# A two-stack transformer kernel on one core: the second stack's attention goes from single heads in loops to pairs of heads, unrolled

## The reference

```python
def mla_attend(q_nope, q_rope, k_nope, k_rope, v):
    s = jnp.einsum('bqhd,bkhd->bhqk', q_nope, k_nope) + jnp.einsum('bqhr,bkr->bhqk', q_rope, k_rope)
    p = jax.nn.softmax(s.astype(jnp.float32) * SOFTMAX_SCALE, axis=-1).astype(v.dtype)
    return jnp.einsum('bhqk,bkhd->bqhd', p, v)
# q: rms_norm(c_q) @ w_q_b   (384 -> 12 heads x 96, of which 32 get a rotary turn)
# k, v: rms_norm(c_kv) @ w_kv_b   (128 -> 12 heads x (64 + 64)), the 32 rotary rows of k are shared
mix_l = jnp.concatenate([four_l, att_l], axis=-1) @ w_out[l]   # four_l: 2-D DFT of 256 channels
```

## Time and profile before

| | us |
|---|---|
| median of three runs | 3974.38 (3973.16 to 3976.8) |
| profiled execution, its own time | 3969.17 |
| its span | 3967.4 |
| TensorE busy | 3636.3 (92%) |
| VectorE busy | 2221.1 (56%) |
| ScalarE busy | 1364.0 (34%) |
| GpSimd busy | 190.7 (5%) |
| mean granted TensorE clock | 0.956 |

### The profile page before, as it was taken

One profiled execution on the slowest core, in us unless ns is written; L12 is line 12 of the kernel. 1 busy time (PEld: TensorE's weight loads), 2 busy tenths in 40 slices (PEclk: granted clock), 3 DMA queues, 4 the chain that ended last, 5 costly groups with the idle time before them and its releaser, 6 DMA issues.

```text
span 3967.4 us, 53234 instructions
## 1 busy us (share of the span) xinstructions
PE 3636.3 (92%) x19180; PEld 2914.2 (73%) x19180; DVE 2221.1 (56%) x3260; ACT 1364.0 (34%) x2104; POOL 190.7 (5%) x157
## 2 busy tenths in 40 slices
PE   8988999999998899999967998899999879879997
PEld 6755787888786578788846775688888657657876
DVE  7864456445686544744566553563535665545445
ACT  5544433222445443322212334142323233324322
POOL 2300000000230000000000000000000000000000
PEclk9988999999998999999978998999999989989998
DMA  3233332222223323222211001111111110112221
GB/s 131 85 139 120 115 113 100 96 95 95 85 86 139 139 100 113 98 95 98 94 58 53 22 21 49 43 53 64 64 64 64 54 64 22 49 64 85 93 87 74
DMA packets 44792, 325.32 MB, mean 82 GB/s; under 512 B 5088, under 2 KB 5344, under 8 KB 6112
## 3 DMA queue, kind: packets, MB, share of 16 engines
q1 hardware_dynamic: 43920, 315.88, 21.9%
q10 hardware_dynamic: 720, 7.40, 0.5%
HBM read 321.16 MB, written 2.10 MB: 81 GB/s over the span
## 4 chain that ended last, share of the span: by engine, by line
PE 76%; DVE 12%; ACT 5%; issue 3%; DVEq 3%; DMA 1%; ACTq 0%; SPq 0%
PE psum L663 10%; PE psum L665 10%; PE psum L664 10%; PE psum L1000 10%; PE psum L1002 10%; PE psum L1001 10%; PE psum L1113 3%; PE psum L1088 3%; ACT whi L1223 2%; PE psum L1099 2%; DVE wlo L1616 2%; DVE MA L1743 2%; PE psum L704 2%; PE psum L767 1%; PE psum L719 1%
## 5 line engine op out<-in xcount | busy, mean ns | idle before, releaser
L1223 ACT ACTIVATE whi<-wst 128x2048 fp32r<-128x2048 f32 x248 | 473.7, 1910 | 787.2 <-PE psum L1002 384.2
L1616 DVE TENSOR_TENSOR wlo<-wst,whi 128x2048 fp32r<-128x2048 f32 x216 | 495.0, 2291 | 197.5 <-ACT whi L1223 196.1
L663 PE MATMUL psum<-xh,whi 128*128 128x512 f32 x1328 | 525.3, 396 | 35.2 <-issue 15.1
L665 PE MATMUL psum<-xh,wlo 128*128 128x512 f32 x1328 | 519.9, 391 | 0.0
L664 PE MATMUL psum<-xl,whi 128*128 128x512 f32 x1328 | 519.7, 391 | 0.0
L1000 PE MATMUL psum<-xh,whi 128*128 128x512 f32 x944 | 380.4, 403 | 52.7 <-DVE xl L2046 40.1
L1001 PE MATMUL psum<-xl,whi 128*128 128x512 f32 x944 | 373.8, 396 | 0.0
L1002 PE MATMUL psum<-xh,wlo 128*128 128x512 f32 x944 | 373.3, 395 | 0.0
L663 PEld LDWEIGHTS psum<-xh,whi 128*128 128x128 f32 x1328 | 251.1, 189 | 99.2 <-issue 47.9
L665 PEld LDWEIGHTS psum<-xh,wlo 128*128 128x128 f32 x1328 | 251.0, 189 | 53.2
L664 PEld LDWEIGHTS psum<-xl,whi 128*128 128x128 f32 x1328 | 251.2, 189 | 52.6 <-issue 1.0
(11 more groups left out here) (300 smaller groups left out, 6570.7 us busy)
## 6 DMA issues: line engine op xcount, KB each, us to landing
wst<-weights SPq DMA_DIRECT2D x296, 1024.0 KB, 4.8
dft<-c_dft ACTq DMA_DIRECT2D x2, 2688.0 KB, 9.0
hT<-x_t SPq DMA_DIRECT2D x4, 512.0 KB, 7.5
out<-hT SPq DMA_DIRECT2D x1, 2048.0 KB, 6.3
masks<-c_masks SPq DMA_DIRECT2D x1, 1024.0 KB, 12.4
cT<-ctx_t ACTq DMA_DIRECT2D x1, 1024.0 KB, 6.4
ropes<-c_ropes ACTq DMA_DIRECT2D x1, 512.0 KB, 7.1
sm<-small ACTq DMA_DIRECT2D x1, 314.0 KB, 2.8
```

Of the source, the lines that this page charges most:

```text
L663: pe.matmul(ps[bank][:, :], w_hi, rh[:, k + k0, :], start=n == 0, stop=False)
L665: last = pe.matmul(ps[bank][:, :], w_lo, rh[:, k + k0, :], start=False, stop=n == len(kts) - 1)
L1223: act.activation(m.whi[:, slot, :], m.wst[:, slot, :], ACT.Copy).then_inc(s.hi_ready, 1)
L1616: TT(m.wlo[:, slot, :], m.wst[:, slot, :], m.whi[:, slot, :].bitcast(F32), ALU.subtract).then_inc(s.lo_ready, 1)
```

## The change

Attention goes by units of two heads and 128 queries, written out instead of looped (24 units with 768 keys a layer, 12 with 256 keys in layer 0). A pair's projections are six steps in layer 0 and five in layer 1 (K, QA, KV, QB, V, QC); those of the next pair are issued at the middle or the end of units of this one, through psum bank 7. Both heads' 64 k rows fill one product; v is 128 columns wide. TensorE reads q in place. The scores are moved to SBUF by the reduction of the first stack. The weighted product has v as weights and gives the output with features on the partitions, which VectorE divides into OT2. One slab holds four heads' weights instead of two slabs; splits of coming slabs stand behind even pairs. ScalarE starts the load of the DFT matrices in the last pair's first unit (p = 5, n = 0). O2, its transposes, ot2, qs2 and GpSimd's copies are gone, and ScalarE makes the heads' high parts between its copies of the channel DFT.

```diff
-S2_WIN, S2_HG, S2_FOUR, S2_WOUT, S2_FFN, SLABS2 = 0, 4, 10, 12, 16, 50
+S2_WIN, S2_HG, S2_FOUR, S2_WOUT, S2_FFN, SLABS2 = 0, 4, 7, 9, 13, 47
+PROJECTED = {0: ("K", "QA", "KV", "QB", "V", "QC"), 1: ("K", "QA", "KV", "QB", "V")}
+BY_ACT, BY_DVE = ("K", "QA", "KV", "QB"), ("K", "QA", "QB", "V", "QC")
+PROJECT_AT = {0: {(0, "mid"): 0, (0, "end"): 1, (1, "mid"): 2, (1, "end"): 3, (2, "mid"): 4, (3, "end"): 5},
+              1: {(0, "mid"): 0, (0, "end"): 1, (1, "mid"): 2, (1, "end"): 3, (2, "mid"): 4}}
+def turn_ring_2():
...
+    for l in range(DEPTH):
+        for u in range(len(UNITS2[l]) + 1):
+            if u < len(UNITS2[l]):
+                for c in range(blocks2(l, u) // 4):
+                    chunk[l, u, c] = len(chunk)
+                    place_(("T", l, u, c), "ACT" if c else "DVE")
+            if u:
+                place_(("R", l, u - 1), "ACT")
...
 TensorE
+                def project(p, n):
+                    name = PROJECTED[l][n]
...
+                        bank = 7
+                        pe.wait_ge(s.p2_dve, projected_by(BY_DVE, l, p, n))
+                        pe.wait_ge(s.p2_act, projected_by(BY_ACT, l, p, n))
...
+                    if name[-1] == "V":
+                        blocks, c0 = (range(QB), 0) if name == "V" else (range(QB, 6), 2 * P)
+                        col = 1792 + (p % 2) * P
+                        w_hi, w_lo = (w_[:, slot, col:col + P] for w_ in (m.whi, m.wlo))
+                        for i, blk in enumerate(blocks):
+                            o = out[:, c0 + i * P:c0 + (i + 1) * P]
+                            h, t = (x[:, blk * P:(blk + 1) * P] for x in (m.ckvh, m.ckvl))
+                            pe.matmul(o, h, w_hi, start=True, stop=False)
+                            pe.matmul(o, h, w_lo, start=False, stop=False)
+                            last = pe.matmul(o, t, w_hi, start=False, stop=True)
+                def logits(u, par):
+                    p, qb, side = units[u]
+                    if unit0 + u:
+                        pe.wait_ge(s.max2_ready, 2 * (unit0 + u - 1) + par + 1)
...
+                        last = pe.matmul(ps[2 * par + c // 512][:, 0:w], m.Q4[0:QH, at, q0:q0 + P],
+                                         m.K4[0:QH, at, side * T + c:side * T + c + w], start=True, stop=True)
+                def weighted(u):
...
+                    for b in range(n):
+                        c, par = b // 4, b % 2
...
+                        mm = pe.matmul(ps[6][VH * par:VH * (par + 1), 0:P], m.V4[:, 4 * side + b // 2, col:col + VH],
+                                       m.PT2[:, CHUNK2[l, u, c] % 5, (b % 4) * P:(b % 4 + 1) * P],
+                                       start=b < 2, stop=b >= n - 2)
+                def denominators(u):
...
+                        last = pe.matmul(ps[bank][VH * par:VH * (par + 1), 0:P],
+                                         m.rden2[:, c:c + 1].broadcast_to([P, VH]), ident, start=True, stop=True)
+                for u in range(len(units) + 1):
...
+                    if u + 1 < len(units):
+                        logits(u + 1, 0)
+                    if u < len(units):
+                        turn(u, 0)
+                    if u + 1 < len(units):
+                        logits(u + 1, 1)
+                    if u < len(units) and blocks2(l, u) > 4:
+                        turn(u, 1)
+                    if here["mid"] is not None:
+                        project(p + 1, here["mid"])
+                    if u < len(units) and blocks2(l, u) > 8:
+                        turn(u, 2)
+                    if u:
+                        weighted(u - 1)
+                        denominators(u - 1)
+                    if here["end"] is not None:
+                        project(p + 1, here["end"])
 ScalarE
+                for u in range(len(units) + 1):
...
+                    if u + 1 < len(units):
+                        exponential(u + 1, 0)
+                    if u < len(units) and blocks2(l, u) > 4:
+                        copy(u, 1)
+                    if here["mid"] is not None:
+                        projected(p + 1, here["mid"])
+                    if u + 1 < len(units):
+                        exponential(u + 1, 1)
+                    if u < len(units) and blocks2(l, u) > 8:
+                        copy(u, 2)
+                    if u:
+                        denominators(u - 1)
+                    if here["end"] is not None:
+                        projected(p + 1, here["end"])
+                    if n == len(SIDES2[l]) - 1 and p % 2 == 0 and p < PAIRS2:
+                        next_group(p + 1)
+                    if p == PAIRS2 - 1 and n == 0:
+                        act.dma_start(m.dft[:, :], io["c_dft"]).then_inc(s.dft_in, 16)
...
                             act.activation(m.AB[:, b, c, :], ps[4 + n % 2][:, 0:2 * P], ACT.Copy
                                            ).then_inc(s.ab_copied, 1)
+                            if n - n0 < len(heads):
+                                head(n - n0)
 VectorE
+                def maximum(u, par):
+                    w, unit, at = blocks2(l, u) // 2 * P, unit0 + u, 2 * (u % 2) + par
+                    if u >= 2:
+                        dve.wait_ge(s.t2_done, RING2["T", l, u - 2, blocks2(l, u - 2) // 4 - 1] + 1)
+                    dve.wait_ge(s.l2_done, 2 * unit + par + 1)
+                    nc.vector.tensor_tensor_reduce(
+                        m.S2[:, at, 0:w], psum[:, 1024 * par:1024 * par + w], m.none[:, 0:1].broadcast_to([P, w]), -1.0,
+                        -TAKEN, ALU.add, ALU.min, m.nmax2[:, at:at + 1]).then_inc(s.max2_ready, 1)
+                for u in range(len(units) + 1):
...
+                    if u + 1 < len(units):
+                        maximum(u + 1, 0)
+                    if u < len(units):
+                        reciprocals(u)
+                        copy(u)
+                    if u + 1 < len(units):
+                        maximum(u + 1, 1)
+                    if here["mid"] is not None:
+                        projected(p + 1, here["mid"])
+                    if u:
+                        normalized(u - 1)
+                    if here["end"] is not None:
+                        projected(p + 1, here["end"])
+                    if n == len(SIDES2[l]) - 1 and p % 2 == 0 and p < PAIRS2:
+                        next2(S2_HG + p // 2)
```

More of the change, by code:

```diff
@@ L1127, in _ @@
[L1127 to L1136 removed]
+                units, unit0 = UNITS2[l], UNIT2[l]
@@ new lines, in _ @@
+                pe.wait_ge(s.acc_free, tl["four"] - FREE_OFF + 4)
+                for par in range(2):
+                    logits(0, par)
+                for u in range(len(units) + 1):
+                    p, n = divmod(u, len(SIDES2[l]))
+                    here = {place_: PROJECT_AT[l].get((n, place_)) if p + 1 < PAIRS2 else None
+                            for place_ in ("mid", "end")}
+                    if u + 1 < len(units):
[15 more added lines that the diff above has]
+                        project(p + 1, here["end"])
@@ new lines, in _ @@
+                for n in range(len(PROJECTED[l])):
+                    projected(0, n)
+                for par in range(2):
+                    exponential(0, par)
+                for u in range(len(units) + 1):
+                    p, n = divmod(u, len(SIDES2[l]))
+                    here = {place_: PROJECT_AT[l].get((n, place_)) if p + 1 < PAIRS2 else None
+                            for place_ in ("mid", "end")}
+                    if u + 1 < len(units):
[16 more added lines that the diff above has]
+                        act.dma_start(m.dft[:, :], io["c_dft"]).then_inc(s.dft_in, 16)
@@ L1547, in _, with head @@
+                act.wait_ge(s.o2_ready, unit0 + len(units))
+                heads = [(j, side, w, c0) for j in range(6) for side, w, c0 in lat_con]
+                def head(h):
+                    j, side, w, c0 = heads[h]
+                    act.activation(x_dst(side)(2 + j), m.OT2[:, j, c0:c0 + w], ACT.Copy).then_inc(s.oth_ready, 1)
+                n0 = 0 if l == 0 else 12
                 n, f = (0, 0) if l == 0 else (12, 4)
@@ new lines, in normalized @@
+                def normalized(u):
+                    p, qb, side = units[u]
+                    c0 = side * T + qb * P
+                    dve.wait_ge(s.pv2_done, 2 * (CHUNK2[l, u, blocks2(l, u) // 4 - 1] + 1))
+                    copied2(dve, RING2["R", l, u])
+                    TT(m.OT2[:, p, c0:c0 + P], ps[6][:, 0:P], m.Rs2[:, u % 2, :], ALU.mult).then_inc(s.o2_ready, 1)
+                for n in range(len(PROJECTED[l])):
+                    projected(0, n)
+                for par in range(2):
+                    maximum(0, par)
```

419 lines of the change are left out of this document (185 added, 234 removed).

## The result

The changed kernel takes 3866.06 us (median of four runs, 3861.55 to 3877.32). The kernel before took 3973.77 beside it (3970.72 to 3976.8). The ratio is 0.9736, its 95% interval 0.9720 to 0.9753: faster by 2.6%. The forecast was 3914 with a range from 3875 to 3955, so the sign was right and the gain was forecast at a little over half of what came. The profiled execution took 3869.55.

What follows compares the result with a forecast made beforehand. TensorE, busy 92%, was taken as the bound. Layer 0's 264.8 us, context DFT's 1.5, layer 1's 217.5 and 12 of waits made 495.8 for 556.6: 60.8 off 3974.4 gives 3914, range 3875 to 3955.

Steps and rivals of the forecast that it cites:

- the DFT's lead: Eight channel-DFT steps before each layer's first position-DFT product, with ScalarE's high parts behind copies: 8.2 and 7.6 us.
- The unit: Attention for two heads, 128 queries and 768 keys: 6.02 us each, 24 a layer, where two old items take 6.58.
- third turn: TensorE's last transposing of four exponential blocks in a 768-key unit: starts 0.1 us late, behind VectorE's copy.
- Waits that a walk misses: Allowance for unseen waits in the units: 0.2 us each for 60 units, 12 us, bounds 0 and 28.
- the 1 us a pair behind the context units: Layer 0, little work between logits and first turn: 1 us added a pair, 6 in all.
- v: Projection of v by 128-column split products: 0.16 us each, 18 a pair, 2.9 us a pair.
- The ends: Layer ends: output transposes leave; DFT steps 8.2 and 7.6 us, context's DFT 1.5 more, filling and draining 6.5 a layer.
- The splits: Three weight-slab splits a layer behind even pairs delay the third turn: 3.5 us each, 10.5 a layer, bounds 0 and 5.
- Rival A: More gained: v's products at 0.117 us (-9.3), no extra waits (-12), splits at half (-10.5): 3882; chance 0.16.
- Rival B: Copies bound at places: 0.47 us a unit (+16), v at 0.229 (+15), splits at 5 (+9): 3954; chance 0.13.
- Rival C: Gaps in the units lower TensorE's granted clock to 0.86: 1.3 us more each, 62 over 48; slower, chance 0.05.
- D: Weighted products of paired heads don't overlap: half passes at 0.107 us add 61 us, 3974, no change; chance 0.02.

## Why the prediction was wrong

The mechanisms were those forecast: TensorE bound, VectorE and ScalarE beside it, the two heads in two halves. What failed are the sizes. The kernel with GpSimd's splits gives the terms without disturbance. Units and projections are counted from their spacing, the DFT's lead is read, and filling and draining is what remains: layer 1 is 138.5 for the units, 43.1 for projections, 6.3 for the DFT's lead and 7.4 for filling and draining, 195.3 in all. In layer 0 a pair takes 37.5 us, of which 23.1 are four units and 9.3 projections, so 5.1 are left for its two context units: 138.5 + 30.6 + 55.7 + 6.1 + 3.5 = 234.4. Against the forecast's 474.8 without splits the two are 45.1 less:

- **The unit.** 6.02 was taken, 5.77 came: 12 us over 48. The third turn was not late. VectorE's copy ended 0.2 us before it, as each operation starts some 0.08 us before the one before ends in its record, and the logits' passes are 1.29 a head and not 1.35, which had a part of the row's joint in it. The half passes (0.057 for 0.058), the changes of mode (0.27 to 0.30 for 0.29) and the reduction (a median of 956 ns for 0.96 us) were right.
- **Waits that a walk misses.** 12 us with bounds 0 and 28 were taken over from the first stack, where they stand beside work of another kind; in the middle of the layers they were 0. Of the 1 us a pair behind the context units, 6 in all, 2.5 came: a context unit is 2.55 for 2.34. The first came from rows of other work and the second from no row.
- **v.** 0.16 us was chosen between 0.117, the nearest row, and 0.22 made of two passes of another kind. It is 0.111: 10.6 us over 216. The range of bounds was fair, and the choice went away from the row of the same kind.
- **The ends.** The DFT's lead was 6.1 and 6.3 for 8.2 and 7.6, 3.4 in all. ScalarE's copies of the heads did not delay the steps; nor did they in the context's DFT, for which 1.5 stood in the sum (from the first stretch's end to the second's start it is 779.8 us after and 779.6 before). Filling and draining, 6.5 a layer, were 3.5 and 7.4.
- **The splits** went the other way. The longest wait was 3.6, as forecast (3.5), but the six were 15.6 us for 21 forecast. Five of them are followed by work at a lowered clock, up to 8.6 us of it at half, and that step the prediction did not price at all: 29.1 for 21.

In sum 45.1 - 8.1 = 37. The steps that failed are thus the walk's third turn and logits (12 us), the allowance for unseen waits (12 and 3.5), v's price (10.6) and, the other way, the splits without their clock (8.1). Rival A had the right three terms and the right sign for two: v and the extra waits came as it said; the splits did not halve. It would have been 3882, still 16 above, as it left the unit and the ends alone.

Rival B, the copies as the bound, did not come, and the rule of TensorEngine Tiling (Array Packing) of the Trainium skill, under PSUM Bottleneck (packing speeds the products and not the evacuation, which may become the bottleneck), is not borne out by this change: outside the splits TensorE's waits are some 11 us in both stretches, nearly all of them in the first and the last units of a layer or at its ends. But the kernels with v for four heads show how near it is: 11 us taken from TensorE's products came back, 6.6 of them as listed waits for the same copies.

Rival C, the clock, was rated for the units and came at the splits: some 12 us of busy time, with 0.97 and 0.98 over the stretches, above the 0.94 that the prediction named as its failure. D is refuted by the run that builds it.

The prediction priced the change as removed passes. The experiment with the projections together shows that the passes stay close only by the order of projections between units: with one bank, losing it costs 134 us, more than the whole gain, and leaves the time of the kernel before (1.0006). Of this order the prediction weighed one place alone, a rotation behind a unit (20 times 1 us if uncovered), and not the waits for the one bank and the clock behind each.

## What to carry to other kernels

Where a walk through the queues says that an engine is full, forecast that, and keep allowances for unseen waits in the range and out of the sum: here two of them, 18 us in all, were 15.5 of the 45 us by which the undisturbed terms were too long. Price the stalls of TensorE with work at half clock behind them, which here nearly doubled them (15.6 us of waits, 29 in time, though one of the six cost only itself), and look for an idle engine for the long operation that causes it: six passes on GpSimd in place of VectorE gave 25 us. And before shortening a product, ask what it covers: v's projection at half the products gained nothing, as the third turns then waited for VectorE's copy.

## What the runs showed of the hardware

- A change from 128-column to 64-column weights and back costs 0.27 to 0.30 us in all.
- Half passes in two column halves overlap fully (0.057 us each), in the same half not at all (0.107), though 64 columns are loaded and not 128.
- A split product of 128 columns takes 0.111 us, one of 256 takes 0.117 and one of 512 0.229: under 256 almost nothing is gained by being narrow.
- A VectorE copy of 128x256 from SBUF to SBUF took 0.27 us, and 4.35 when it met GpSimd's pass of 4.53 us, from whose end it went on. In the kernel with GpSimd's splits, where every VectorE operation that stood beside a pass read psum or a few columns (the reductions, copies, divisions and reciprocals), nothing of the kind appeared; the rotation's additions, which read SBUF twice, never fell beside one.
- VectorE operations with two operands in SBUF are held up in the same way. The first stack shows it, where GpSimd splits slabs in the kernel before and after alike. Below, an addition that takes 0.69 us elsewhere takes 5.03, and a product that takes 0.68 takes 2.43; both ended 0.54 us after GpSimd's pass.

```profile
52.08 4.57 POOL L667 TENSOR_TENSOR wlo<-wst,whi 128x2048 fp32r<-128x2048 f32 x1 [10.29 <-ACT whi L1296]
52.16 5.03 DVE L1745 TENSOR_TENSOR AK<-xc,xs 64x512 f32<-64x512 f32 x1
...
104.67 4.88 POOL L667 TENSOR_TENSOR wlo<-wst,whi 128x2048 fp32r<-128x2048 f32 x1 [7.27 <-ACT whi L1296]
107.66 2.43 DVE L1742 TENSOR_TENSOR xs<-xs,sinR 128x512 f32<-128x512 f32 x1
```

- SBUF — State Buffer of the Trainium skill, under SBUF: two separate sides, states as an exclusive lock a pair of SBUF ports that VectorE and GpSimd share. On VectorE's side it is taken by an operation in a two-port mode, or by one with two SBUF inputs beside a GpSimd operation that reads SBUF; whichever engine starts second waits for the whole of the other's operation. The copy's 4.35 us agrees with the first case, the 5.03 and 2.43 with the second, each begun while GpSimd's pass ran.
